# Routing in two parts: the last three tiles' table entries by 0/1 products instead of scatters

## The reference

```python
t = x.reshape(-1, D)
g_logits = t @ w_rg + b_rg                      # 4 groups
grp = argmax(g_logits); p_grp = softmax(g_logits)[grp]
e_in = (t @ w_re + b_re).reshape(-1, 4, 4)[grp] # 4 experts of that group
top_p, top_i = top_k(softmax(e_in), 2)
weights = p_grp * top_p / sum(top_p)
for e in range(16):
    h = silu(t @ w_gate[e]) * (t @ w_up[e])
    y = y + combine[:, e:e+1] * (h @ w_down[e])
```

## Time and profile before

| | before |
|---|---|
| median of 3 runs | 1027.12 us (1024.5 to 1027.66) |
| the profiled execution's own time | 1022.0 us |
| its span | 1020.2 us |
| PE busy | 908.5 us, 89% of the span |
| DVE busy | 617.0 us, 60% |
| ACT busy | 528.9 us, 52% |
| POOL busy | 247.0 us, 24% |
| last output projection ends | 509.24 us |
| first expert matmul starts | 558.05 us |

### The profile page before, as it was taken

How to read it: one execution, slowest core, us unless ns; L and a number is a source line. 1 busy time by engine, 2 the same in 40 slices (tenths; PEclk the granted TensorE clock), 3 DMA queues, 4 the chain that set the end, 5 groups by cost and what they waited for, 6 DMA issues and landing times.

```text
span 1020.2 us, 16968 instructions
## 1 busy us (share of the span) xinstructions
PE 908.5 (89%) x5042; PEld 750.6 (74%) x5043; DVE 617.0 (60%) x1245; ACT 528.9 (52%) x953; POOL 247.0 (24%) x368
## 2 busy tenths in 40 slices
PE   3889999999999957899921999999999999999994
PEld 2679888888898846788711787787787877778773
DVE  2756566666666573434567636645759399754892
ACT  2374654646637380222133635644658488663881
POOL 3101101011010100000054234324315245423352
PEclk9999999999999958899955999999999999999997
DMA  8620010100100322344552977768769799966963
GB/s 260 225 66 22 22 42 0 41 21 21 41 0 22 105 102 90 138 146 141 206 207 79 371 217 265 231 180 258 265 169 372 208 332 394 373 178 210 318 253 62
DMA packets 58123, 169.68 MB, mean 166 GB/s; under 512 B 12745, under 2 KB 15089, under 8 KB 58097
## 3 DMA queue, kind: packets, MB, share of 16 engines
q1 hardware_dynamic: 50384, 143.13, 39.1%
q0 software_dynamic: 7712, 26.24, 10.6%
HBM read 142.96 MB, written 26.38 MB: 166 GB/s over the span
## 4 chain that ended last, share of the span: by engine, by line
PE 71%; DVE 9%; issue 7%; ACT 5%; POOL 4%; DMA 3%; DVEq 0%; ACTq 0%; SPq 0%; POOLq 0%
PE bank_j L913 14%; PE bank_j L915 13%; PE bank_j L914 13%; DVE w_low L1674 6%; PE bank_j L1009 5%; PE bank_t L907 4%; PE bank_j L1020 3%; PE bank_o L1000 3%; ACT w_high L653 2%; PE bank_t L993 2%; POOL table L558 2%; DMA PT<-in_w_in_dram 1%; PE bank_s L915 1%; PE bank_s L913 1%; PE bank_o L913 1%
## 5 line engine op out<-in xcount | busy, mean ns | idle before, releaser
L913 PE MATMUL bank_j<-w_high,rows_high 128*128 128x512 f32 x640 | 260.7, 407 | 20.2 <-DVE w_low L1674 9.2
L914 PE MATMUL bank_j<-w_low,rows_high 128*128 128x512 f32 x640 | 251.8, 393 | 0.0
L915 PE MATMUL bank_j<-w_high,rows_low 128*128 128x512 f32 x640 | 251.7, 393 | 0.0
L913 PEld LDWEIGHTS bank_j<-w_high,rows_high 128*128 128x128 f32 x640 | 121.4, 190 | 61.7 <-DVE w_low L1674 21.2
L545 POOL TENSOR_TENSOR tick<-mhalf 1x1 f32<-1x1 f32 x146 | 84.0, 578 | 272.7 <-ACT lg L850 151.6
L915 PEld LDWEIGHTS bank_j<-w_high,rows_low 128*128 128x128 f32 x640 | 121.4, 190 | 26.7
L914 PEld LDWEIGHTS bank_j<-w_low,rows_high 128*128 128x128 f32 x640 | 121.8, 190 | 22.5
L1674 DVE TENSOR_TENSOR w_low<-w_res,w_high 128x1024 fp32r<-128x1024 f32 x96 | 112.7, 1216 | 13.8 <-ACT w_high L653 13.8
L653 ACT ACTIVATE w_high<-w_res 128x1024 fp32r<-128x1024 f32 x96 | 96.2, 1060 | 8.0 <-PE bank_j L915 8.0
L907 PE MATMUL bank_t<-ident,hn 128*128 128x128 f32 x328 | 45.2, 284 | 36.2 <-DMA hn<-ffn_in,row_g 22.6
L907 PEld LDWEIGHTS bank_t<-ident,hn 128*128 128x128 f32 x328 | 40.1, 147 | 41.3 <-issue 37.1
(11 more groups left out here) (307 smaller groups left out, 1775.9 us busy)
## 6 DMA issues: line engine op xcount, KB each, us to landing
w_res<-in_w_gate_dram SPq DMA_DIRECT2D x48, 512.0 KB, 5.1
w_res<-in_w_up_dram SPq DMA_DIRECT2D x48, 512.0 KB, 5.5
bias<-in_w_down_dram SPq DMA_DIRECT2D x32, 512.0 KB, 5.6
slot_b<-in_w_gate_dram SPq DMA_DIRECT2D x16, 512.0 KB, 5.7
PT<-in_w_up_dram SPq DMA_DIRECT2D x16, 512.0 KB, 6.0
gmix<-in_w_down_dram SPq DMA_DIRECT2D x16, 512.0 KB, 5.5
h<-in_w_down_dram SPq DMA_DIRECT2D x16, 512.0 KB, 7.3
hn<-in_x_dram SPq DMA_DIRECT2D x8, 512.0 KB, 3.3
```

Source lines behind the costliest of these rows:

```text
L913: pe.matmul(out_, ah, bh, start=start, stop=False)
L914: pe.matmul(out_, ah, bl, start=False, stop=False)
L915: return pe.matmul(out_, al, bh, start=False, stop=stop)
```

## The change

Tiles 0 to 4 are now routed early, tiles 5 to 7 late. The early routing is cut in pieces that VectorE runs in tiles 6 and 7 of the output projection (`groups` in tile 6 ahead of L1587, `masks` behind it, the rest in tile 7), its constants in tile 5; for that, tiles 5, 6 and 7 are written out behind the loop. Only their ten scatters remain, and SP reads the table after them. For the late tiles VectorE writes, for each of six pairs of tile and choice, a 0/1 matrix of the row in the table (128 x 128) and two matrices of the column (128 x 130), one multiplied by the row number less its preset, one by the weight; TensorE sums their products in one bank (`late_slots`), and VectorE adds the bank to `rows`. The table holds floats now; each pick on GpSimd turns one to an integer, and the first one's copy is on VectorE. The first tile's gather no longer waits for a copy of GpSimd. The columns of the tiles (`columns`) are computed behind `rows_lo`. VectorE's first three splits and ScalarE's first conversions move ahead of the late routing; ScalarE's squares of tile 7 move ahead of its copy of the router parts. The methods `groups`, `masks`, `weights` and `slots` of the class hold the statements of `route` in their old order (payload integers excepted), and are left out below.

```diff
-        table = nc.dram_tensor("table", (P * TCOLS, 2), I32, kind="Internal").ap()
+        table = nc.dram_tensor("table", (P * TCOLS, 2), F32, kind="Internal").ap()
...
-        rows = sb("rows", [P, TCOLS, 2], I32)
+        rows = sb("rows", [P, TCOLS, 2])
...
+        EARLY = TILES - 3
+        ints = sb("ints", [P, TCOLS + TILES], I32)
+        slot_1h = [hn[:, i * P:(i + 1) * P] for i in range(6)]
...
             one(0, 0, True, False)
-            with eng.Fori(0, (TILES - 2) // 2) as pair:
+            with eng.Fori(0, (TILES - 4) // 2) as pair:
                 one(2 * pair + 1, 1, False, False)
                 one(2 * pair + 2, 0, False, False)
-            one(TILES - 1, (TILES - 1) % 2, False, True)
+            for t in range(TILES - 3, TILES):
+                one(t, t % 2, False, t == TILES - 1)
 
...
-            sp.wait_ge(st_rows, 16 * 2 * TILES)
+            sp.wait_ge(st_rows, 16 * 2 * EARLY)
...
-            chain(pool.memset(rows[:, :, 1], 0))
-            pool.iota(rows[:, :, 0], pattern=[[0, TCOLS]], base=S, channel_multiplier=1).then_inc(pool_const, 1)
+            chain(pool.iota(rows[:, :, 1].bitcast(I32), pattern=[[0, TCOLS]], base=S, channel_multiplier=1))
+            chain(pool.tensor_copy(rows[:, :, 0], rows[:, :, 1].bitcast(I32)))
+            pool.memset(rows[:, :, 1], 0.0).then_inc(pool_const, 1)
-            pool.iota(ints[:, 0:NI], pattern=[[1, NI]], base=0, channel_multiplier=0)
-            pool.iota(ints[:, NI:], pattern=[[P, TILES]], base=0, channel_multiplier=1)
+            pool.iota(ints[:, 0:TCOLS], pattern=[[1, TCOLS]], base=0, channel_multiplier=0)
+            pool.iota(ints[:, TCOLS:], pattern=[[P, TILES]], base=0, channel_multiplier=1)
...
-            def scatter_rows(a, b, n):
-
-                pool.wait_ge(dve_pay, n)
-                for t in range(a, b):
+            def scatter_early():
+
+                pool.wait_ge(st_tab, 16)
+                pool.wait_ge(dve_pay, 1)
+                for t in range(EARLY):
...
-                    pool.wait_ge(st_tab, 16)
-                    scatter_rows(0, TILES - 2, 1)
+                    scatter_early()
             tiles2(pool, body2, chain, 1)
-
-            scatter_rows(TILES - 2, TILES, 2)
-            pool.wait_ge(st_rows, 16 * 2 * TILES)
 
...
-            pool.wait_ge(pe_h2T, TILES)
-            pool.wait_ge(ld_rows, 16)
-
-            pool.tensor_copy(row_g[:, :], rows[:, 0, 0:1]).then_inc(pool_rowg, 1)
-            pool.wait_ge(pool_rowg, 1)
+            pool.wait_ge(dve_rows, 1)
             gather()
-            pool.wait_ge(dve_tab, 1)
+            pool.wait_ge(dve_cols, 1)
             pool.wait_ge(ld_g, 16)
             pick(row_g, 1)
-            pool.wait_ge(pool_rowg, 2)
+            pool.wait_ge(pool_rowg, 1)
             pool.wait_ge(pe_mx, 1)
             gather()
             pool.wait_ge(st_h, 16 * TILES)
+            pool.wait_ge(dve_tab, 1)
 
             def tile(t):
                 pwait(ld_g, 16 * t + 32)
                 pick(row_g, t + 2)
-                pwait(pool_rowg, 2 * t + 3)
...
-                    route_exp(TILES - 2, 1)
+                    route_exp(EARLY, 1)
                 if not first:
                     h2T_half(t - 1)
                 if not last:
                     mix_high(t + 1, 1 - u)
-                if not first:
+                if not first and not last:
                     router_parts(t - 1)
                 act.wait_ge(dve_h, t + 1)
                 act.activation(junk, xin[:, u, :], ACT.Square, accum_out=ssh[:, :]).then_inc(act_ssh, 1)
+                if last:
+                    router_parts(t - 1)
 
             tiles2(act, body2)
-            h2T_half(TILES - 1)
-            router_parts(TILES - 1)
 
 
...
-            route_exp(2, 2)
             act.wait_ge(pe_y1, TILES)
-            for i in range(PIECES):
+            for i in range(4):
+                split_hi(0, i, None)
+            h2T_half(TILES - 1)
+            split_hi(0, 4, None)
+            router_parts(TILES - 1)
+            for i in range(5, 2 * FC):
+                split_hi(0, i, None)
+            route_exp(TILES - EARLY, 2)
+            for i in range(2 * FC, PIECES):
                 split_hi(0, i, None)
             act.wait_ge(dve_tab, 1)
             rows_hi(0)
...
+            def late_slots():
+
+                pe.wait_ge(dve_h, TILES)
+                n = len(slot_1h)
+                for i in range(n):
+                    pe.wait_ge(dve_onehot, i + 1)
+                    ins = pe.matmul(J1[:, 0:2 * TCOLS], slot_1h[i], col_1h[i], start=(i == 0), stop=(i == n - 1))
+                ins.then_inc(pe_late, 1)
+
...
+                if last:
+                    positions(EARLY, 1)
...
-                    positions(TILES - 2, 1)
...
-            positions(2, 2)
-
+            positions(TILES - EARLY, 2)
+            late_slots()
...
+            def route_constants():
+
+                ids, late_ids = new(TILES), new(TILES - EARLY)
+                chain(dve.tensor_copy(iota_f[:, :], ints[:, 0:TCOLS]))
+                chain(dve.tensor_scalar(iota_m[:, :], iota_f[:, 0:NG], -1.0e4, None, ALU.add))
+                chain(dve.tensor_scalar(strict, tri[:, :], -0.5, None, ALU.is_gt))
+                dve.tensor_tensor(strict, strict, ident[:, :], ALU.subtract)
+                dve.memset(onesm, 1.0)
+                dve.memset(off_e[:, :], 0.0)
+                chain(dve.tensor_copy(ids, ints[:, TCOLS:]))
+                for c in range(2):
+                    dve.tensor_copy(pay[:, :, c, 0], ids)
+                chain(dve.tensor_scalar(late_ids, ids[:, EARLY:], -float(S), None, ALU.add))
+                return late_ids
...
+            class Route:
...
+                def groups(self):
...
+                def masks(self):
...
+                def weights(self):
...
+                def slots(self):
...
+                def payload(self):
+
+                    chain(dve.tensor_scalar(self.dst, self.dst, float(TCOLS), None, ALU.mult))
+                    chain(dve.scalar_tensor_tensor(self.dst, self.col, -float(P * TCOLS - 1), self.dst, ALU.mult, ALU.add))
+                    dve.tensor_copy(desti[:, self.a:self.b, :], self.dst).then_inc(dve_pay, 1)
+
+                def onehots(self, late_ids):
+
+                    T_ = self.T
+                    val = new(2 * T_).rearrange("p (t c) -> p t c", c=2)
+                    chain(dve.scalar_tensor_tensor(self.dst, self.col, -float(P), self.dst, ALU.mult, ALU.add))
+                    tt(val, self.bc(late_ids, 2), self.dst, ALU.subtract)
+                    dve.wait_ge(pe_mixT, TILES)
+                    for t in range(T_):
+                        for c in range(2):
+                            i = 2 * t + c
+                            col = self.col[:, t, c:c + 1]
+                            dve.tensor_scalar(slot_1h[i], iota_f[:, 0:P], self.dst[:, t, c:c + 1], None, ALU.is_equal)
+                            dve.tensor_scalar(col_1h[i][:, 0:TCOLS], iota_f[:, :], col, val[:, t, c:c + 1],
+                                              ALU.is_equal, ALU.mult)
+                            dve.tensor_scalar(col_1h[i][:, TCOLS:], iota_f[:, :], col, pay[:, self.a + t, c, 1:2],
+                                              ALU.is_equal, ALU.mult).then_inc(dve_onehot, 1)
 
...
+            early, late = Route(0, EARLY, 1), Route(EARLY, TILES, 2)
+
             def body2(t, u, first, last):
-                if last:
-
-                    dve.wait_ge(dve_rl, TILES - 2)
-                    route(0, TILES - 2, 1)
+                prep = isinstance(t, int) and t == TILES - 3
...
+                if prep:
+                    late.ids = route_constants()
+                if mid:
+                    early.groups()
+                if last:
+                    early.weights()
+                    early.slots()
+                    early.payload()
                 dve.wait_ge(pe_y1, t + 1)
                 dve.tensor_tensor(xin[:, u, HALF:], J1[:, :], xin[:, u, HALF:], ALU.add).then_inc(dve_h, 1)
+                if mid:
+                    early.masks()
                 dve.wait_ge(pool_rh, t + 1)
                 dve.wait_ge(dve_h, t + 1)
...
+            split_lo(0, 0)
             h2T_half(TILES - 1)
+            for i in range(1, 3):
+                split_lo(0, i)
             router_logits(TILES - 1)
 
 
-            dve.wait_ge(dve_rl, TILES)
-            route(TILES - 2, TILES, 2)
+            late.groups()
+            late.masks()
+            late.weights()
+            late.slots()
+            late.onehots(late.ids)
+            dve.wait_ge(ld_rows, 16)
+            dve.wait_ge(pe_late, 1)
+            chain(dve.tensor_tensor(rows[:, :, :], rows[:, :, :], J1[:, 0:2 * TCOLS].rearrange("p (c a) -> p a c", c=2),
+                                    ALU.add))
+            dve.tensor_copy(row_g[:, :], rows[:, 0, 0:1]).then_inc(dve_rows, 1)
 
             one = slice(0, 1)
...
```

(38 more changed lines are left out.)

148 lines of the change are left out of this document (67 added, 81 removed).

## The result

| | before | after |
|---|---|---|
| median | 1027.34 us (1024.5 to 1027.66, 4 runs) | 1013.53 us (1009.82 to 1015.7, 4 runs) |
| ratio to before | | 0.9869, 95% interval 0.9844 to 0.9895 |
| span of the profiled execution | 1020.2 us | 1008.0 us |
| last projection ends to first expert matmul | 509.24 to 558.05, 48.8 us | 509.54 to 543.95, 34.4 us |

The forecast was 1014.3 us. The profiled execution's own time was 1009.82 us. Both profiled executions are faster than their kernel's median; their spans differ by 12.2 us, the medians by 13.8.

The account below looks back on a forecast made before the run. The bound was TensorE's 48.8 us gap before the first expert matmul, with VectorE's routing, then GpSimd's scatters and copy ending last. Terms: -13.8 + 0.5 + 0.5 = -12.8, giving 1014.3 us against the median; range 1011.5 to 1016.5.

Parts of the forecast that it names:

- Early routing at no cost, L1593 of tile 7 ending at 514.3: VectorE, tiles 5 to 7: routing pieces fit into idle times, so tile 7's scaling ends 6.0 us earlier.
- Last logits at 519.45, nothing charged for the splits put between: Behind tile 7's scaling: the old distance of 5.15 us stays, with three splits and ScalarE's conversions fitting into waits.
- Late routing, rounded column at 528.1: VectorE behind the last logits: routing three tiles costs one addition of 0.2 us more than two.
- 0/1 matrices 0.65 us a triple, products 5.6 us at the lower clock: Late tiles: VectorE's eighteen operations, then TensorE's 12 instructions at 0.47 us each, clock 1.2 GHz, ending at 534.8.
- Table not last: GpSimd's ten scatters: the tenth starts at 525.7, reading ends at 530.0, 4.8 us ahead of the products.
- Gather at 535.8, first expert matmul at 544.3: Behind the sum into `rows`: without GpSimd's 5.79 us copy, the first expert matmul comes 13.8 us earlier than 558.05.
- Start +0.5: Kernel start: GpSimd's added conversion of 130 columns and longer iota delay VectorE's first copy by 0.5 us.
- rival A: GpSimd's first executed copy costs 5.8 us anywhere, so the new conversion near 8 us pays it; 1019.5 us, chance 0.20.
- Second tile +0.5, ends 0 and +3.5: Second tile's gather: deferred columns and splits 8 to 11 delay GpSimd's pick and issue, costing 0.5 us.
- rival B: A burst of splits holds GpSimd's pick throughout; TensorE waits 3.2 us at the second tile; 1017.0 us, chance 0.16.
- the two theories of the 5.79 us: GpSimd's copy L607 ahead of the first gather: held by VectorE's burst of splits, or costly when GpSimd first reaches it.
- theory 1a: Only a burst of VectorE's splits without gaps holds GpSimd's copy; with gaps it takes at most 1.2 us.

Follow-up runs that it names:

- a_route_one_piece: Changed kernel with the early routing in one piece at the head of the last tile, its positions behind tile 7's second half; 1018.07 us, ratio 0.9972.
- a_copy_on_pool: Changed kernel with the first tile's row numbers copied by GpSimd again, behind the sum into `rows`; 1014.64 us, ratio 0.9887.
- a_wait_pick: Changed kernel with VectorE waiting for GpSimd's first pick ahead of its last four splits (8 to 11); 1008.69 us, ratio 0.9848.
- a_gap_splits: Changed kernel with each of VectorE's last four splits waiting for the end of the one before; 1008.87 us, ratio 0.9846.
- b_gap_splits: Kernel before the change, with each of its eight splits ahead of the first expert waiting for the one before; 1021.01 us, ratio 0.9957.
- a_control: The changed kernel itself, unedited, run again as partner on the same chip; 1016.01 us, ratio 0.9907.
- a_columns_first: Changed kernel with `columns()` ahead of `dve_tab` again, as before the change; 1013.64 us, ratio 0.9908.
- a_late_scatter: Changed kernel with tiles 5 to 7 put into the table by six scatters again, without 0/1 matrices and products; 1016.49 us, ratio 0.9943.

## Why the prediction was right, and where it was not

By its own steps, against the profile after:

- *Early routing at no cost, L1593 of tile 7 ending at 514.3.* Measured 514.36, by the rows at 499.40, 508.83 and 512.34 above. Undoing it costs 5.1 us at the last sum, against the 5.25 of the step (514.75 to 509.5).
- *Last logits at 519.45, nothing charged for the splits put between.* 519.40. ScalarE's four conversions ended at 515.36, 1 us ahead of the end of tile 7's transposes (four times the 1.06 of the row would be 515.9, not 515.6). That nothing had to be charged is right; that it came out to 0.05 us is luck, since the same code put them anywhere within 1.5 us in the seven kernels above.
- *Late routing, rounded column at 528.1.* 528.36; from the logits on the third tile cost some 0.3 more than the one addition charged.
- *0/1 matrices 0.65 us a triple, products 5.6 us at the lower clock.* The triples took 0.71 (528.79, 529.51, 530.22 and on). The products took 4.28, because the granted clock rose from 1.2 to 2.4 GHz while they ran (windows of the profile: 0.50 from 520 to 528, 0.62 from 528 to 534). This term was mis-sized by 1.3 us, partly offset by a first product that began 0.6 us later than forecast. The size is not a constant of the kernel either: from the first product to the sum into `rows` it is 4.38 us in the profile after, 4.60 to 5.02 in seven others with the products, and 5.65 in a_route_one_piece, where the clock did not rise.
- *Table not last.* Ten scatters; the fourth was held beside a split (2.02 us), the last started at 526.86 instead of 525.7. SP issued the read of the table at 529.0 and it landed 1.9 us later, some 3 us ahead of the sum at 534.12, where 4.8 were forecast.
- *Gather at 535.8, first expert matmul at 544.3.* 535.58 and 543.95. By the 0.87 us between the two profiles of this kernel, a hit to 0.35 is closer than the prediction could know.
- *Start +0.5.* VectorE's first copy starts at 11.24 instead of 10.77, and the conversion of 130 columns takes 0.30 us. This alone refutes rival A: it is the first conversion or copy that GpSimd executes, and a_copy_on_pool and a_wait_pick say the same of the later ones.
- *Second tile +0.5, ends 0 and +3.5.* This term was mis-sized, and the cause was rival B's. The columns were done at 547.6, where 548.9 was forecast, so the pick was not late before it met the burst. From first matmul to second transposes it is 16.19 us after; 14.33 and 14.28 in the two kernels whose pick isn't held; 13.42 before. So the hold cost 1.9 us. The other 0.9 is there without the hold. More than half of it is the clock: it rises 5.7 to 6.0 us behind the first expert matmul instead of 4.6, and until then matmuls start 0.43 us apart instead of 0.23. The last 0.3 are spread over short steps ahead of the transposes. The charge should have been 2.8 instead of 0.5.

Rows of GpSimd's timeline of the changed kernel (the first conversion, the held scatter), and of VectorE's (the first copy, the first 0/1 matrix):

```profile
7.87 0.30 POOL L536 CAST rows<-rows 128x130 f32<-128x130 int32 x1
...
518.20 2.02 POOL L568 DMA_INDIRECT table<-pay,desti  x1 [0.30 <-issue]
```

```profile
11.24 0.28 DVE L1265 COPY osg<-bank_x 8x128 f32<-8x128 f32 x1 [11.09 <-POOL vm L547]
...
528.79 0.29 DVE L1408 TENSOR_SCALAR hn<-iota_f,qk 128x128 f32<-128x128 f32 x1
```

Added up: the first expert matmul is 14.1 us earlier (-13.8 forecast plus the 0.5 of the start: -13.3), the second tile gives 2.8 back, and behind the second tile's transposes the span is 0.9 us shorter (447.9 against 448.7): -12.2. That last part lies inside what the profiled executions differ by. The forecast was -12.8: two errors of opposite sign, 0.8 too little gained and 2.3 too little charged, and the 0.9 that was not forecast. That they nearly cancel is luck.

The weighing of the two theories of the 5.79 us went wrong in one respect. The prediction held the row at 584.97 (1.15 us beside a split) against a hold by the burst. Both are true: ahead of the experts a copy waits for the last split, in the expert loop it waits for one. VectorE's timeline beside the copy at 584.97, in the kernel before:

```profile
583.73 1.21 DVE L1674 TENSOR_TENSOR w_low<-gmix,w_high 128x1024 fp32r<-128x1024 f32 x1
584.86 2.35 DVE L1674 TENSOR_TENSOR w_low<-bias,w_high 128x1024 fp32r<-128x1024 f32 x2
```

That a wait for the end of the split before frees the copy ahead of the experts was shown (a_gap_splits, b_gap_splits). Why the copy gets in after one split in the loop was not: the waits there have register values, but the splits start 1.13 us apart, as closely as in the burst, and the rows show no gap. So theory 1a, which put the loop down to gaps made by register operations, is proven only for the place where the waits were added. Of the rule of the Trainium skill (SBUF — State Buffer, Who interferes with whom), that a VectorE instruction with two SBUF inputs and a GpSimd instruction reading SBUF exclude each other, the measured holds are an instance, but the length of the copies' hold ahead of the experts is the burst's and not the instruction's.

**A version that beats both.** a_wait_pick and a_gap_splits are the changed kernel with one more line. They stand at 0.9848 (0.9826 to 0.9869) and 0.9846 (0.9828 to 0.9863) of before, against 0.9907 (0.9892 to 0.9923) for the changed kernel on the same chip. The medians are 7.2 us apart; the distances account for 3.8 to 4.9 of it (end of span 510.7 against 507.0 and 505.9). What is left lies outside the stage: it started 3 us earlier in the profile of a_wait_pick than in a_control's, and at the same time in that of a_gap_splits. Nothing shows that the edit did this, so only the 3.8 to 4.9 are credited to it.

## What to carry to other kernels

A chain of short operations costs nothing where it is cut to the idle times of its engine, and the products that it needs must then be moved ahead of the long ones on TensorE too: that part was worth about as much as the removed scatters. When a producer is moved behind other work, look at who waits for it on every queue and at what has been put beside that waiter; here a pick that used to run in quiet came to stand beside a burst of splits. A GpSimd copy that is on the path should not meet a burst of VectorE's two-input instructions: here a wait of each for the end of the one before cost 0.1 us an instruction and made the copy 3.4 to 5.4 us shorter.

## What the runs showed of the hardware that was not expected

*A burst holds a copy of GpSimd to its end.* 5.78 us (before), 3.59 (seven kernels), 5.00 (a_columns_first), each ending with the last split; 0.18 to 0.43 where the splits start some 0.1 us further apart or nothing runs beside it.

*It does not hold the issue of an indirect DMA so long.* That is held as well, 2.02 instead of 0.96 us beside splits, 1.51 and 1.46 in the two kernels with the earlier pick. But it is let in at the end of the split that runs, also inside a burst. In a_wait_pick the issue at 549.19 is over at 550.70, 0.84 us behind the end of the first split, while the others follow until 553.3. In a_late_scatter it is the same (timelines of GpSimd and VectorE): the first of the two splits ends near 517.15, the issue at 517.99, the second split at 518.29.

```profile
516.55 1.44 POOL L568 DMA_INDIRECT table<-pay,desti  x1 [0.30 <-issue]
```

```profile
515.94 2.35 DVE L1674 TENSOR_TENSOR w_low<-w_res,w_high 128x1024 fp32r<-128x1024 f32 x2
```

Why the copy isn't let in there stays open.

*A wait of 2 us can also cost the clock.* In a_control the wait at the second tile is no longer than in the profile after (2.06 and 2.09 us), but the transposes behind it take 1.96 us instead of 1.09, and from their start to that of the third tile's transposes it is 20.6 us instead of 19.05. TensorE's windows in a_control (length, busy of PE, PEld, DVE, ACT, POOL, clock, DMA, GB/s):

```profile
559.00:561.00 2.00, 2.00 (x12) 1.59 (x10) 0.88 (x3) 0.99 (x3) 0.00 (x0) 1.00 1.03 414
561.00:563.00 2.00, 0.37 (x2) 0.00 (x0) 1.40 (x2) 0.79 (x2) 0.00 (x0) 1.00 1.00 393
563.00:565.00 2.00, 1.57 (x8) 1.57 (x9) 0.00 (x0) 0.00 (x0) 0.56 (x3) 0.58 1.03 420
565.00:567.00 2.00, 2.00 (x7) 1.67 (x6) 0.00 (x0) 0.00 (x0) 1.17 (x2) 0.56 0.72 293
```

```profile
563.43 1.96 PE L917 MATMUL bank_t<-ident,hn 128*128 128x128 f32 x8 [2.06 <-DMA hn<-ffn_in,row_g]
```

The granted clock fell from 2.4 GHz to 1.2 GHz for some 3 us behind the idle stretch. It did so in five of the seven kernels of the study that have this wait (2.06 to 3.16 us long), the control among them, and not in a_route_one_piece (2.79) nor in the first profile after (2.09). In those five the third tile comes 1.2 to 1.6 us later. So against a_control, removing the wait gave 3.5 us from the first expert matmul to the third tile's transposes, 1.9 by the wait and the rest by the clock. Why it fell in some and not in others stays open.
